# Hybrid decoder step with expert retrieval: a gather ring of five slots instead of six, with the residual rows and the second gate kept in SBUF

## The reference, cut to what matters

```python
    mix = jnp.concatenate([hA.reshape(B, T, W_A), att.reshape(B, T, W_B)], axis=-1).astype(x.dtype) @ w_out
    x = x + gate1 * mix
    h2 = rmsnorm(x, norm2_g) * (1 + scale2) + shift2
    x = x + gate2 * peer(h2, peer_wq, peer_keys, peer_u, peer_v)

def peer(h, w_q, sub_keys, u_tab, v_tab):
    def block(xblk):
        qh = (xblk @ w_q).reshape(PEER_BLOCK, PEER_HEADS, 2, PEER_DQ // 2)
        s = jnp.einsum('nhpd,pkd->nhpk', qh, sub_keys).astype(jnp.float32)
        sv, si = lax.top_k(s, K)
        ...
        gate = jax.nn.softmax(fv, axis=-1)
        act = jax.nn.gelu(jnp.einsum('nd,nhkd->nhk', xblk, u_tab[eidx]), approximate=False)
        return jnp.einsum('nhk,nhkd->nd', (gate * act).astype(xblk.dtype), v_tab[eidx])
```

## Time and profile before

| what | value |
|---|---|
| median of three runs | 4178.97 us |
| the profiled execution's own time | 4189.1 us |
| its span | 4187.3 us |
| POOL, gathers (L1160) | 1088, the first issued at 1067.5 us |
| moved by DMA in all | 1420.21 MB, of it 1200.70 MB in the queue of the gathers |
| PE, DVE, ACT, POOL busy | 84%, 57%, 39%, 31% of the span |
| mean granted TensorE clock | 0.94 of full speed |

### The profile page before, as it was taken

One profiled execution on the slowest core, in us unless ns is written; L12 is line 12 of the kernel. 1 busy time (PEld: TensorE's weight loads), 2 busy tenths in 40 slices (PEclk: granted clock), 3 DMA queues, 4 the chain that ended last, 5 costly groups with the idle time before them and its releaser, 6 DMA issues.

```text
span 4187.3 us, 38259 instructions
## 1 busy us (share of the span) xinstructions
PE 3507.9 (84%) x12228; PEld 1772.0 (42%) x12228; DVE 2391.9 (57%) x5587; ACT 1616.4 (39%) x4381; POOL 1283.8 (31%) x1204
## 2 busy tenths in 40 slices
PE   7299999678689879978987897898889789889877
PEld 1065665445335334433533453453445344425321
DVE  1044554326548746944874595478548656947744
ACT  0033233123443453454345444443543453333333
POOL 0000000011334433423442343344344334435433
PEclk9699999679799999998998999899999999999999
DMA  9796011875799999999998999899999999999998
GB/s 377 266 339 217 26 44 36 169 251 200 307 377 413 416 358 402 413 364 349 414 416 325 398 413 397 321 401 416 397 386 400 412 386 396 400 368 410 413 408 366
DMA packets 241245, 1420.21 MB, mean 339 GB/s; under 512 B 42963, under 2 KB 65875, under 8 KB 93315
## 3 DMA queue, kind: packets, MB, share of 16 engines
q0 software_dynamic: 168768, 1200.70, 71.4%
q1 hardware_dynamic: 68692, 132.05, 9.9%
q10 hardware_dynamic: 3584, 85.01, 5.7%
HBM read 1385.48 MB, written 98.73 MB: 354 GB/s over the span
## 4 chain that ended last, share of the span: by engine, by line
PE 32%; DMA 25%; DVE 11%; ACT 8%; issue 2%; POOL 1%; SPq 0%; ACTq 0%; POOLq 0%; DVEq 0%
PE psum L1335 21%; DMA mem<-in_experts,mem 20%; DVE mem L1631 6%; PE psum L1252 4%; PE psum L1234 3%; DMA mem<-key_cols 3%; ACT L1441 2%; DVE mem L1497 1%; ACT mem L1445 1%; DVE mem L1496 1%; ACT mem L1442 1%; DMA mem<-qkv_rows 1%; ACT L1362 1%; PE psum L1190 1%; ACT mem L1441 1%
## 5 line engine op out<-in xcount | busy, mean ns | idle before, releaser
L1335 PE MATMUL psum<-mem 128*128 128x512 f32 (+1 forms) x4352 | 2136.4, 624 | 376.9 <-ACT mem L1445 374.8
L1160 POOL DMA_INDIRECT mem<-in_experts,mem x1088 | 1218.0, 1120 | 1882.0 <-PE psum L1335 1814.7
L1631 DVE CUSTOM_DVE_ANT_0 mem<-mem 128x1024 f32<-128x1024 f32 x1088 | 1321.4, 1221 | 705.8 <-DMA mem<-in_experts,mem 694.5
L1335 PEld LDWEIGHTS psum<-mem 128*128 128x128 f32 (+1 forms) x4352 | 774.5, 193 | 1458.0 <-ACT mem L1445 733.4
L1441 ACT ACTIVATE mem<-mem 128x1 f32<-128x1 f32 x1088 | 219.3, 202 | 1579.1 <-DVE mem L1631 1574.6
L1445 ACT ACTIVATE mem<-mem 128x128 f32<-128x128 f32 (+1 forms) x1088 | 434.3, 399 | 35.7
L589 PE MATMUL psum<-mem 128*128 128x512 f32 (+3 forms) x864 | 342.7, 548 | 11.0 <-ACT mem L554 9.8
L1442 ACT ACTIVATE mem<-mem 128x1 f32<-128x1 f32 x1088 | 320.4, 294 | 35.3
L1252 PEld LDWEIGHTS psum<-mem 128*128 128x128 f32 x2304 | 274.4, 191 | 45.1 <-issue 41.7
L1252 PE MATMUL psum<-mem 128*128 128x128 f32 (+1 forms) x2304 | 282.1, 275 | 2.5 <-ACT mem L1391 2.5
L589 PEld LDWEIGHTS psum<-mem 128*128 128x128 f32 (+1 forms) x864 | 148.8, 190 | 178.4 <-issue 164.6
(11 more groups left out here) (259 smaller groups left out, 2577.6 us busy)
## 6 DMA issues: line engine op xcount, KB each, us to landing
out_k_s<-in_cache_k ACTq DMA_DIRECT2D x8, 4080.0 KB, 104.5
out_v_s<-in_cache_v ACTq DMA_DIRECT2D x8, 4080.0 KB, 117.2
mem<-in_w_ada SPq DMA_DIRECT2D x12, 2048.0 KB
mem<-mod_rows SPq DMA_DIRECT2D x34, 512.0 KB
mem<-in_experts,mem POOLq DMA_INDIRECT x1088
mem<-in_keys_t POOLq DMA_DIRECT2D x16, 1024.0 KB, 6.5
mem<-in_vals POOLq DMA_DIRECT2D x16, 1024.0 KB, 7.7
mem<-in_w_in ACTq DMA_DIRECT2D x8, 1796.0 KB, 40.5
```

The source lines that it names most:

```text
L1160: pool.indirect_dma_start(out=ring[:, g % N_SLOTS].rearrange("p a n -> p (a n)"), out_offset=None, in_=ins["experts"][:, :], in_offset=bas ...
L1335: mm = nc.tensor.matmul(psum[0:r, half], diag[:, g % 4, 0:r], ring[:, g % N_SLOTS, 1, half * 512:(half + 1) * 512], start=c == 0, stop=c = ...
L1631: v.tensor_tensor_reduce(row, row, h2[i % 2], 1.0, 0.0, ALU.mult, ALU.add, dots[:, c:c + 1]).then_inc(sig["dots"], 1)
```

## The change

The ring gets five slots. In the 2048 floats of the sixth stand a second x1 buffer (`x1_odd`) and a buffer of its own for the second gate (`gate2`). Tiles take turns between the two x1 buffers, so that x1 stays in SBUF until `finish` needs it: the write to `x_rows`, the wait for it and the load back are gone. The second gate is the same row of numbers for all eight prompt tiles; it is loaded once for tile 0, and once more for tile 8, whose tokens have gates of their own. Tile 1's `x` lands where the sample attention has worked, and its load waits for that to be done. All instructions on PE, DVE, ACT and POOL stay, in the same order.

```diff
-N_SLOTS = 6
+N_SLOTS = 5
...
+    ring_at = work.at
     ring = work.take(N_SLOTS, 2, D)
-    x1 = work.take(D)
+    x1_odd, gate2 = work.take(D), work.take(D)
+    ring_end = work.at
+    x1 = (work.take(D), x1_odd)
     mod_a = work.take(D)
...
-    s_ring = Region(ring.rearrange("p s a n -> p (s a n)"), 0, N_SLOTS * 2 * D)
+    s_ring = Region(mem, ring_at, ring_end)
...
         def y_in(i):
             r = rows_of(i)
-            sp.dma_start(mod_a[0:r], mod_rows(5, i)).then_inc(sig["gate2_in"], 16)
-            sp.dma_start(x1[0:r], scratch["x1"].ap()[rows_at(i), :]).then_inc(sig["x1_back"], 16)
+            if i == 0:
+                sp.dma_start(gate2, mod_rows(5, 0)).then_inc(sig["gate2_in"], 16)
+            if i == NT:
+                sp.dma_start(gate2[0:r], mod_rows(5, NT)).then_inc(sig["gate2_in"], 16)
...
-            sp.dma_start(x1[0:r], ins["x"][rows_at(n), :]).then_inc(sig["x1_in"], 16)
+            if n == 1:
+                sp.wait_ge(sig["s_att"], DB)
+                sp.wait_ge(sig["s_out0"], 32 * DB // 2)
+                sp.wait_ge(sig["s_out1"], 32 * DB // 2)
+            sp.dma_start(x1[n % 2][0:r], ins["x"][rows_at(n), :]).then_inc(sig["x1_in"], 16)
...
             sp.dma_start(mod_a[0:r], mod_rows(3, n)).then_inc(sig["shift2_in"], 16)
-            sp.dma_start(scratch["x1"].ap()[rows_at(n), :], x1[0:r]).then_inc(sig["x1_out"], 16)
             sp.wait_ge(sig["h2"], n + 1)
-            sp.wait_ge(sig["x1_out"], 16 * (n + 1))
...
         def finish(i):
             r = rows_of(i)
             dve.wait_ge(sig["acc_read"], 2 * i + 2)
-            dve.wait_ge(sig["gate2_in"], 16 * (i + 1))
-            dve.wait_ge(sig["x1_back"], 16 * (i + 1))
-            chain.link(v.tensor_tensor(mix[0:r], mix[0:r], mod_a[0:r], ALU.mult))
-            v.tensor_tensor(mix[0:r], mix[0:r], x1[0:r], ALU.add).then_inc(sig["y"], 1)
+            dve.wait_ge(sig["gate2_in"], 16 if i < NT else 32)
+            chain.link(v.tensor_tensor(mix[0:r], mix[0:r], gate2[0:r], ALU.mult))
+            v.tensor_tensor(mix[0:r], mix[0:r], x1[i % 2][0:r], ALU.add).then_inc(sig["y"], 1)
```

More of the change, by code:

```diff
@@ L218, in layer @@
             "mix": nc.dram_tensor("mix_rows", [NTOK, D], F32),
-            "x1": nc.dram_tensor("x1_rows", [NTOK, D], F32),
         }
@@ L1382, in search @@
                 act.wait_ge(sig["x1"], n + 1)
-                chain.link(a.activation(mix[0:r], x1[0:r], ACT.Square, accum_out=ss[0:r]))
+                chain.link(a.activation(mix[0:r], x1[n % 2][0:r], ACT.Square, accum_out=ss[0:r]))
                 chain.link(a.activation(ln[0:r], ss[0:r], ACT.Ln, scale=1.0 / D, bias=eps[0:r]))
@@ L1514, in search @@
                     chain.wait()
-                    op = v.tensor_tensor(x1[R, cols], x1[R, cols], mod_a[R, cols], ALU.add)
+                    op = v.tensor_tensor(x1[n % 2][R, cols], x1[n % 2][R, cols], mod_a[R, cols], ALU.add)
                     if half == 1:
@@ L1522, in search @@
                 dve.wait_ge(sig["gain2_in"], 16 * (n + 1))
-                chain.step(v.scalar_tensor_tensor(out=h2[n % 2][R], in0=x1[R], scalar=rs[R], in1=mod_b[R], op0=ALU.mult, op1=ALU.mult))
+                chain.step(v.scalar_tensor_tensor(out=h2[n % 2][R], in0=x1[n % 2][R], scalar=rs[R], in1=mod_b[R], op0=ALU.mult, op1=ALU.mult))
             if c == at["h2"] + 1:
```

## The result

The changed kernel takes 4278.09 us (median of four runs, 4266.23 to 4285.05), the kernel before beside it 4179.05 us (4177.4 to 4180.96): a ratio of 1.0232, with a 95% interval from 1.0204 to 1.026. It is 99 us slower. The forecast was 4172.6 us with a range up to 4192: the wrong sign.

The account below looks back on a forecast made before the run. The third stage was taken as close to DMA-limited, though not everywhere. Saved bytes -28.8, projection and residual step +19.9, attention heads +2.5, search nothing: -6.4 us from 4178.97, so 4172.6 us; own range 4164 to 4180, 8-in-10 range 4150 to 4192.

Parts of the forecast that it names:

- (c): The search, picks 70 to 109: DMA engines full, so five slots suffice and the missing slot costs nothing.
- those 2.2 us: In the search, the spare time of a five-slot loop: 12.9 us available against 10.7 needed, before VectorE's own delays.
- need of 6.23 us to landing: Time from a gather's issue to VectorE's reading where nothing else is in the way, taken from one undisturbed pick.
- third rival: The search becomes limited by slots through VectorE's waits and longer POOL issues: 24 us more, 4197 us; chance 0.17.
- (a): Output projection and residual step: the missing slot costs 2.49 us in each of eight windows, 19.9 us (0 to 27.3).
- One gather: The loss assumed per window at the output projection and residual step: one gather's DMA time, 2.49 us.
- hole at pick 60: After the residual step: a 2 to 3 us gap in the DMA rate, expected in the changed profile.
- (b): Attention heads, tiles 0 to 4: missing slot against sooner loads of keys, a loss of 2.5 us (-12.5 to +12.5).
- second rival: Attention heads: queues take turns, so loads of keys come no sooner; 12.5 us lost there, 4182.5 us; chance 0.16.
- The bytes, -28.8: DMA time saved by dropping x1's write and load back and the second gate's loads: 23 transfers x 1.25 us.
- first rival: The sixth slot is worth nothing, so all 28.8 us are gained: 4150 us; chance 0.15.
- quiet loop: One slot's cycle in the last window, without attention or search: forecast 12.47 us with five slots, some 8.0 to landing.

Follow-up runs that it names:

- experiment 8: The changed kernel (five slots, residual rows and gate kept on chip) with four slots instead: 4648.56 us, ratio 1.1123.
- the control with the moves: The kernel before with three buffers moved, six slots and the transfers of residual rows and gate through memory kept: 4171.56 us, ratio 0.9982.

## Why the prediction was wrong

- **The step that failed is (c): "I cost it at nothing; its cover is those 2.2 us".** It measured 49 us (868.0 against 818.9 with six slots and no trips), 4 to 8 us in each of the eight windows. The cover was compared with delays on average, and with a need of 6.23 us to landing that experiment 8 puts at 5.5 to 7.5 us even with no other work beside it. In the search a slot is delayed by VectorE, PE and POOL's issue, one after the other and unevenly, as the hole above shows. The losses are not a sum of shares: against 814.4 us with both kinds of work out, VectorE's search alone costs 39 us (853.0), PE's products alone 66 (880.4), both together 54 (868.0). Either is enough to overrun what five slots spare, and only without both does the loss go. With six slots both cost just 16 us (818.9 against 802.6). Why the holes aren't made up later is argued and not tested: the DMA engines and PE (busy 97.65 of 100.8 us before) are both almost full.
- **The third rival had the right place and, in the main, the right mechanism**, but it named VectorE's waits and the issues, not PE, and gave it 24 us and a chance of 0.17. Its "against", that such a wait shrinks by itself when rows come later, didn't hold: with PE's products out VectorE's search still costs 39 us.
- **Two stretches were not priced at all.** "Three places in a window have to be priced" leaves out picks 0 to 11 and 110 to 127. Five slots cost 7.9 and 13.0 us there (against six and no trips), and 8.6 and 12.0 with both kinds of work out. What delays them no run tells.
- **(a), 19.9 us, was mis-sized.** Between six and five slots without trips, picks 36 to 56 differ by 31.2 and picks 57 to 69 by 14.0: 45 us, above the upper bound of 27.3. "One gather" was reckoned at one place of a window; but slots are delayed all along the projection, and without PE's products (and VectorE's search) the sixth slot is worth 11.5 us in picks 36 to 56 instead of 31.2. The hole at pick 60 is there as forecast, though these 13 picks of tile 4 take 35.7 us with six slots and no trips as well; stretches at tile 4's residual step after, columns as in the earlier trace rows:

```profile
2782.00:2785.00 3.00, 3.00 (x7) 1.28 (x6) 2.88 (x4) 0.90 (x3) 1.21 (x1) 0.86 0.78 328
2785.00:2787.00 2.00, 2.00 (x6) 0.86 (x5) 0.75 (x3) 0.90 (x3) 1.03 (x2) 1.00 0.79 213
2787.00:2790.00 3.00, 3.00 (x11) 1.46 (x10) 1.50 (x3) 0.90 (x3) 2.44 (x2) 1.00 0.97 374
2790.00:2793.00 3.00, 2.69 (x10) 1.18 (x8) 0.44 (x2) 1.39 (x4) 0.94 (x1) 1.00 1.01 360
```

  Against 421 GB/s these 11 us move 1.02 MB too little, 2.4 us. The issues of picks 60 and 61 there, against the earlier trace rows:

```profile
2783.47 1.21 POOL L1166 DMA_INDIRECT mem<-in_experts,mem  x1 [6.83 <-PE psum L1341]
2785.18 0.94 POOL L1166 DMA_INDIRECT mem<-in_experts,mem  x1 [0.51 <-PE psum L1341]
```

  And their dots:

```profile
2789.21 1.23 DVE L1636 CUSTOM_DVE_ANT_0 mem<-mem 128x1024 f32<-128x1024 f32 x1 [1.50 <-DMA mem<-in_experts,mem]
2793.06 1.23 DVE L1636 CUSTOM_DVE_ANT_0 mem<-mem 128x1024 f32<-128x1024 f32 x1 [2.62 <-DMA mem<-in_experts,mem]
```

  Pick 60 came 5.74 us after its issue, as the reckoning had it (6.23); but pick 61 followed 3.85 us later, not 2.49. Behind this hole the reckoning's full rate from one gather to the next was not reached.
- **(b)** can't be settled: five slots cost 13.6 us in the heads' picks against the kernel with six and no trips, where +2.5 (-12.5 to +12.5) was forecast, but kernels that should agree there differ by 16. The two longest loads of keys in the chain of waits of tile 4, after, against the 11.51 and 14.51 of the earlier trace rows:

```profile
2643.14 6.25 DMA mem<-key_cols
...
2667.48 13.56 DMA mem<-key_cols
```

  One came sooner and one nearly as late. But before the change, with six slots, the two lengths stand side by side too, in the windows of tiles 2 and 3:

```profile
1845.70 13.34 DMA mem<-key_cols
...
2252.51 6.21 DMA mem<-key_cols
```

  So neither "sooner" nor the second rival's rule on turns is borne out.
- **The bytes, -28.8**, were right as DMA time (26 measured with six slots and PE's and VectorE's work out), but have no price of their own: 14 us with six slots and that work in place, 49 with five slots. The first rival falls with the slot's price.
- **What the profile was to show:** the quiet loop of 12.47 us with 8.0 from issue to landing, and the 12.6 MB, were right. VectorE's idle time after the residual step is back at 1.25 us for pick 59, but 1.50 and 2.62 us for picks 60 and 61. Windows 0 to 6 shorter were not right. The mark set for (c), the search over 99 us in tile 4 and a share below 1.00, is met: 108.7 us and 0.99.
- In sum the sixth slot was priced at 22.4 us and is worth 120: 98 of the 105.5 us between forecast and result. The bytes gave 14 instead of 28.8, 15 us more; the difference between the kernel before and the control with the moves, 7.5 us the other way, is within noise.

## What to carry to other kernels

Price a buffer of a ring by the uneven delays of its loop, over all engines that the slot passes and in every stretch of the window, not by the mean slack of a quiet stretch. When looking for what delays it, leave the suspects out together as well as one by one: in the search, the runs with one left out gave back 15 us or nothing, and the run with both gave back all. Read the DMA share together with GB/s by slices: here a share of 0.99 hid 7% of the rate. And look for room before giving up a slot: three buffers whose lives don't overlap made place for both the slot and the rows on chip, which at 4158 us beats either kernel.

## What the runs showed of the hardware

The 8 KB packets of the gathers take 0.31 us each in the trace's DMA records. Of some 4900 in picks 70 to 107 of tile 4, 18 took over 0.5 us before the change, 195 after it and 388 with four slots, on average 0.8 us. That accounts for 0.15 of the 0.21 us by which a pick there is slower after the change. With five slots and both kinds of work out there are 25. That these are the first packets of an engine that had run out is inferred from where they stand, at the holes; it was not measured apart. While such a packet is under way the engine counts as busy, so the share hardly falls, 1.01 to 0.99.
